# The output mixing of a hybrid block: its products in another order, its attention half in three rounded terms, and the first queries at its end

## The reference

```python
h = rms_norm(x, norm1_g);  proj = h @ w_in
y_lru = rg_lru(conv(xr)) * gelu(gate)              # 512 columns
y_fox = forgetting_attention(q, k, v, log_f)       # 512 columns, 8 heads
y_mix = concat(rms_norm(y_lru, gn_lru_g), rms_norm(y_fox, gn_fox_g))
x  = x + y_mix @ w_out                             # the mixing
h2 = rms_norm(x, norm2_g)
x  = x + peer(h2, peer_wq, peer_subkeys, peer_u, peer_v)
return rms_norm(x, final_g)
```

## Time and profile before

| what | value |
|---|---|
| median of 3 runs | 2812.67 us (2809.37 to 2816.16) |
| the profiled execution, whole | 2814.05 us |
| its span in the trace | 2812.3 us |
| PE busy in the span | 2706.6 us, 96% |
| DVE / ACT / POOL busy | 2306.2 / 1250.8 / 1456.7 us |
| instructions | 39998 |
| mixing block, start to the next block's first product | 476.8 to 608.2 us |
| score block, likewise | 608.2 to 830.6 us |

### The profile page before, as it was taken

How to read it: one execution, slowest core, us unless ns; L and a number is a source line. 1 busy time by engine, 2 the same in 40 slices (tenths; PEclk the granted TensorE clock), 3 DMA queues, 4 the chain that set the end, 5 groups by cost and what they waited for, 6 DMA issues and landing times. The chain is left out here.

```text
span 2812.3 us, 39998 instructions
## 1 busy us (share of the span) xinstructions
PE 2706.6 (96%) x14923; PEld 2374.2 (84%) x14923; DVE 2306.2 (82%) x4081; ACT 1250.8 (44%) x2540; POOL 1456.7 (52%) x935
## 2 busy tenths in 40 slices
PE   7999899979999999999999999989999999999998
PEld 6777665459999999999999999987788888878887
DVE  3297795329989989788979797775999999999997
ACT  4244432113332222888888888862222222222222
POOL 1122320004338885566666666662666666657662
PEclk9999899989999999999999999999999999999999
DMA  4110100323238886999999999999999999999995
GB/s 119 44 38 23 60 1 23 90 68 111 63 94 312 297 296 207 358 389 378 388 380 401 380 390 396 389 378 325 382 383 383 386 388 386 386 379 379 391 384 223
DMA packets 332114, 762.66 MB, mean 271 GB/s; under 512 B 23232, under 2 KB 158400, under 8 KB 329360
## 3 DMA queue, kind: packets, MB, share of 16 engines
q0 software_dynamic: 111104, 403.02, 38.3%
q1 hardware_dynamic: 220096, 353.67, 35.5%
q10 hardware_dynamic: 720, 3.41, 0.3%
HBM read 667.73 MB, written 92.27 MB: 270 GB/s over the span
## 5 line engine op out<-in xcount | busy, mean ns | idle before, releaser
L1985 POOL DMA_INDIRECT v_rows<-in_peer_v,row_numbers x336 | 535.6, 1594 | 332.5 <-DVE y_rest L2058 189.2
L1620 PE MATMUL expert_pre<-h2T,wq_then_uT_hi 128*128 128x320 f32 x4096 | 674.1, 314 | 24.5 <-ACT wq_then_uT_hi L1654 22.2
L1734 POOL DMA_INDIRECT u_rows<-in_peer_u,row_numbers x384 | 554.0, 1443 | 246.8 <-DVE row_weights L1754 161.0
L1620 PEld LDWEIGHTS expert_pre<-h2T,wq_then_uT_hi 128*128 128x128 f32 x4096 | 613.0, 189 | 27.3 <-issue 26.9
L2115 PE MATMUL expert_out<-v_hi,w_hi 128*128 128x512 f32 x1280 | 501.2, 392 | 12.7 <-DVE w_lo L2036 12.3
L1754 DVE CUSTOM_DVE_ANT_0 u_rows<-u_rows,h_rows_kept 128x1024 f32<-128x1024 f32 x384 | 488.3, 1300 | 27.8 <-DMA u_rows<-in_peer_u,row_numbers 27.7
L2115 PE MATMUL expert_out<-v_lo,w_hi 128*128 128x512 f32 x1280 | 499.6, 390 | 0.0
L2115 PE MATMUL expert_out<-v_hi,w_lo 128*128 128x512 f32 x1280 | 499.2, 390 | 0.0
L2058 DVE SCALAR_TENSOR_TENSOR y_rest<-v_rows,row_weights,y_rest 128x1024 f32<-128x1024 f32 x256 | 326.4, 1278 | 22.0 <-DMA v_rows<-in_peer_v,row_numbers 20.7
L1620 PE MATMUL expert_pre<-h2T,wq_then_uT_lo 128*128 128x320 f32 x2048 | 343.8, 310 | 0.6 <-POOL wq_then_uT_lo L1723 0.6
L1620 PEld LDWEIGHTS expert_pre<-h2T,wq_then_uT_lo 128*128 128x128 f32 x2048 | 312.4, 189 | 1.0 <-POOL wq_then_uT_lo L1723 0.8
(11 more groups left out here) (325 smaller groups left out, 4177.8 us busy)
## 6 DMA issues: line engine op xcount, KB each, us to landing
wq_then_u<-in_peer_u_turned SPq DMA_DIRECT2D x128, 512.0 KB
pick_memory<-in_peer_v SPq DMA_DIRECT2D x128, 512.0 KB
pick_memory<-acts_dram SPq DMA_DIRECT2D x128, 320.0 KB
acts_dram<-expert_acts SPq DMA_DIRECT2D x124, 320.0 KB
pick_memory<-gates_dram SPq DMA_DIRECT2D x31, 1280.0 KB
gates_dram<-pick_memory SPq DMA_DIRECT2D x19, 2048.0 KB
wq_then_u<-in_peer_wq SPq DMA_DIRECT2D x32, 512.0 KB, 4.0
w_in_columns<-in_w_in SPq DMA_DIRECT2D x20, 512.0 KB, 3.9
```

The source lines that it names most:

```text
L1620: last = nc.tensor.matmul(pre[:, (2 * c + half) % 4, 0:WIDTH], part[:, c % 2, k], m.h2T[:, t, k, HALVES[half]], start=n == 0, stop=n == le ...
L1734: pool.indirect_dma_start(rows[:, k % RING], None, table, bass.IndirectOffsetOnAxis(ap=m.row_of[:, f, slot:slot + 1], axis=0)).then_inc(fe ...
L1985: pool.indirect_dma_start(rows[:, k % ROW_RING], None, d.peer_v, bass.IndirectOffsetOnAxis(ap=m.row_of[:, f, slot:slot + 1], axis=0)).then ...
```

## The change

It gives the two halves different kinds of products, and moves work between three stages:

- The logits' three banks and the bank of the square sums become one PSUM tile of four banks, `m.front`, which the mixing and then the queries use too.
- `w_out` is loaded in attention in two halves. The second half goes to `m.rows`. In the mixing it is split there into `w_hi` (ACT) and `w_lo` (DVE 3 quarters, POOL 1), and then rows of x and new rows take its place.
- PE computes lru(0) in attention's end: 7 of its 8 products ahead of the last square sums, the last one behind them.
- The attention half of each tile is rounded by ACT (`split_fox`) and its rest taken by DVE (`low_fox`), in one buffer each. `out_fox` is then 24 rounded products instead of 8 plain ones.
- The lists of PE, DVE and ACT are interleaved one tile apart instead of two for fox, and the queries 0 and 1 on tiles 0 to 2 are made in the mixing's last two steps. POOL and SP split and load a third group of `peer_wq` there.
- The scores begin with query 2, the subkeys, scores 0 and 1, then query 3.

```diff
 @attend
+                def first_lru(products):
+                    if 0 in products:
+                        pe.wait_ge(m.w_out_in, 32)
+                        pe.wait_ge(gained, CT + 1)
+                        pe.wait_ge(logit_read, turn(FH, 0))
+                    for n in products:
+                        half, c = divmod(n, CT)
+                        last = nc.tensor.matmul(m.front[:, half], m.gateT[:, c, 0:P], m.w_out[:, c, half * HALF:(half + 1) * HALF],
+                                                start=c == 0, stop=c == CT - 1)
+                    return last
...
+                first_lru(range(2 * CT - 1))
                 pe.wait_ge(squared, SUMS)
                 square_sums(squares[:, (SUMS - 1) % 2], 2 * NT)
+                first_lru([2 * CT - 1]).then_inc(m.lru_mixed, 1)
 @mix_out, SP
+                sp.dma_start(gain2[:], d.norm2_g.partition_broadcast(P)).then_inc(m.gains_in, 16)
+                for n in range(2):
+                    sp.dma_start(m.wq[:, n], d.peer_wq[:, n * P:(n + 1) * P].rearrange("(k p) n -> p k n", p=P)
+                                 ).then_inc(m.wq_in[n], 16)
                 for b in range(NT):
-                    if b >= 2:
+                    if b < 2:
+                        m.w_out_lo_done.wait(sp, b + 1)
+                    else:
                         sp.wait_ge(dve4, added(b - 2, X2))
                     sp.dma_start(x_row[:, b % 2], d.x[b * P:(b + 1) * P, :]).then_inc(x_in[b % 2], 16)
...
+                sp.wait_ge(m.wq_lo_done, 1)
+                sp.dma_start(m.wq[:, 0], d.peer_wq[:, 2 * P:3 * P].rearrange("(k p) n -> p k n", p=P)).then_inc(m.wq_in[0], 16)
 @mix_out, ACT
+                def split_fox(b):
+                    if b:
+                        act.wait_ge(fox_mixed, b)
+                    A(fox_hi[:], fox_of(b), ACT.Copy).then_inc(m.fox_hi_done.semaphore, 1)
+
+                act.wait_ge(m.w_out_in, 32)
+                for c in range(CT):
+                    A(w_hi[:, c], m.rows[:, c], ACT.Copy).then_inc(m.w_out_hi_done.semaphore, 1)
+                split_fox(0)
                 act.wait_ge(dve4, 2)
                 A(rgroup[:], rgroup[:], ACT.Sqrt).then_inc(group_root, 1)
                 for b in range(NT):
+                    if b + 1 < NT:
+                        split_fox(b + 1)
                     act.wait_ge(dve4, added(b, X2))
...
 @mix_out, DVE
+                for c in range(BY_DVE):
+                    m.w_out_hi_done.wait(dve, c + 1)
+                    v.tensor_tensor(*split_of(c)).then_inc(m.w_out_lo_done.semaphore, 1)
+                low_fox(0)
...
-                add_groups(0)
-                add_groups(1)
+                add_lru(0)
+                add_lru(1)
+                add_fox(0)
                 for b in range(NT):
+                    if b + 1 < NT:
+                        low_fox(b + 1)
                     normalize(b)
+                    if b + 2 < NT:
+                        add_lru(b + 2)
                     low(b)
-                    if b + 2 < NT:
-                        add_groups(b + 2)
+                    if b + 1 < NT:
+                        add_fox(b + 1)
 @mix_out, PE
+                def mix_fox(b):
+                    m.fox_lo_done.wait(pe, b + 1)
+                    if b == 0:
+                        m.w_out_hi_done.wait(pe, CT)
+                        m.w_out_lo_done.wait(pe, BY_DVE)
+                        m.w_out_lo_pool.wait(pe, CT - BY_DVE)
+                    else:
+                        pe.wait_ge(dve4, added(b - 1, X2))
+                    terms = [(a, of, c) for a, of in ((fox_hi, w_hi), (fox_lo, w_hi), (fox_hi, w_lo)) for c in range(CT)]
+                    for half, cols in enumerate(halves(2)):
+                        for n, (a, of, c) in enumerate(terms):
+                            last = nc.tensor.matmul(out_fox[:, half], a[:, c], of[:, c, cols],
+                                                    start=n == 0, stop=n == len(terms) - 1)
+                    last.then_inc(fox_mixed, 1)
...
-                for b in range(2):
-                    mix_lru(b)
-                    mix_fox(b)
+                mix_lru(1)
+                mix_fox(0)
                 for b in range(NT):
                     if b + 2 < NT:
                         mix_lru(b + 2)
+                    else:
+                        query_of_rows(b + 2 - NT)
                     turn(b)
-                    if b + 2 < NT:
-                        mix_fox(b + 2)
+                    if b + 1 < NT:
+                        mix_fox(b + 1)
 @score, PE
-                for n in range(HP):
+                query_of(2)
+                turn_keys()
+                score_of(0)
+                score_of(1)
+                for n in range(3, HP):
                     query_of(n)
-                    if n == 0:
-                        turn_keys()
-                    else:
-                        score_of(n - 1)
+                    score_of(n - 1)
 @score, ACT
+                query_out(0)
+                query_out(1)
+                split_high(3)
+                for g in range(HP // 4):
+                    act.wait_ge(keys_turned, g + 1)
+                    A(keysT[:, 4 * g:4 * g + 4, :], keys_ps, ACT.Copy).then_inc(keysT_done, 1)
+                scores_out(0)
+                query_out(2)
+                scores_out(1)
+                split_high(4)
```

More of the change, by code:

```diff
@@ L57, in enter, with __init__, wait @@
         self.count, self.base = 0, i * per_pass
+class Counted:
+    def __init__(self, semaphore, base):
+        self.semaphore, self.base = semaphore, base
+    def wait(self, engine, count):
+        engine.wait_ge(self.semaphore, self.base + count)
 def halves(n=2):
@@ L1047, in _, with add_lru @@
                 dve.wait_ge(m.gains_in, 16)
-                def add_groups(b):
+                def add_lru(b):
                     s = b % 2
                     dve.wait_ge(lru_mixed, b + 1)
+                    if b == 0:
+                        m.w_out_lo_done.wait(dve, BY_DVE)
+                    if b == 1:
+                        m.w_out_lo_pool.wait(dve, CT - BY_DVE)
                     dve.wait_ge(x_in[s], 16 * (b // 2 + 1))
@@ L1070, in normalize @@
                     own.link(v.reciprocal(r2[:, b:b + 1], r2[:, b:b + 1]))
[L1071 to L1072 removed]
+                    if b:
+                        dve.wait_ge(h2_turned, b)
                     own.link(v.scalar_tensor_tensor(out=h2_of(b), in0=x2[:, s], scalar=r2[:, b:b + 1],
@@ L1088, in _, with mix_lru @@
-                assert own.count == normalizing(NT)
+                    assert own.count == lowered(b)
+                    if b + 1 < NT:
+                        add_fox(b + 1)
             @block.tensor
             def _(pe):
-                pe.wait_ge(m.w_out_in, 16)
-                def mix(b, to, of, first, which, done):
-                    if b:
-                        pe.wait_ge(dve4, added(b - 1, which))
+                def mix_lru(b):
+                    if b >= 2:
+                        pe.wait_ge(dve4, added(b - 1 if b > 2 else 0, LRU_READ))
@@ L1110, in turn, with query_of_rows @@
                     last.then_inc(h2_turned, 1)
-                for b in range(2):
-                    mix_lru(b)
-                    mix_fox(b)
+                def query_of_rows(n):
+                    pe.wait_ge(m.wq_lo_done, n + 1)
+                    pe.wait_ge(dve4, max(lowered(F - 1), added(NT - 1, LRU_READ)))
+                    terms = [(w, part, k) for w, part in ((m.wq_hi, 0), (m.wq_hi, 1), (m.wq_lo, 0)) for k in range(KT)]
+                    for i, (w, part, k) in enumerate(terms):
+                        last = nc.tensor.matmul(m.front[:, n, 0:F * P], w[:, n % 2, k], m.h2_of_rows[:, part, k],
+                                                start=i == 0, stop=i == len(terms) - 1)
+                    last.then_inc(m.query_done, 1)
+                mix_lru(1)
+                mix_fox(0)
                 for b in range(NT):
@@ L1312, in _ @@
                 sp.dma_start(keys[:], d.peer_subkeys.rearrange("h n c -> n h c")).then_inc(keys_in, 16)
-                for s in range(2, 2 * HP):
+                for s in range(3, 2 * HP):
                     sp.wait_ge(lo_done, s - 1)
@@ L1437, in scores_out @@
                     A(to[:, h % ring, p], score_ps[:, s % 2, tiles.start:tiles.stop], ACT.Copy).then_inc(scores_read, 1)
-                for n in range(HP):
-                    query_out(n)
-                    if n == 0:
-                        for g in range(HP // 4):
-                            act.wait_ge(keys_turned, g + 1)
-                            A(keysT[:, 4 * g:4 * g + 4, :], keys_ps[:], ACT.Copy).then_inc(keysT_done, 1)
-                    else:
-                        scores_out(n - 1)
+                query_out(0)
[8 more added lines that the diff above has]
+                split_high(4)
+                for n in range(3, HP):
+                    query_out(n)
```

(8 more changed lines are left out.)

110 lines of the change are left out of this document (64 added, 46 removed).

## The result

The changed kernel takes **2787.24 us** (median of 4 runs, 2781.68 to 2789.16), the kernel before 2814.01 beside it on the same chip: ratio **0.9905, 95% interval 0.9888 to 0.9922**. The forecast was 2787.0, range 2779 to 2798. The profiled execution took 2781.68 us with a span of 2779.9.

A forecast was written before the change was run, and what follows sets the result against it. PE's list was taken to set the mixing's and score block's ends. From 2814.05 us, 20.0 from the mixing and 6.4 from the scores, 26.4 together, gave 2787.6, stated as 2787 us, range 2779 to 2798.

The forecast's parts named there:

- Attention's end: End of attention: 7 plain products take 6.0 us in PE's wait, square sums 1.8; mixing starts at 476.5 instead of 476.85.
- Entry: Start of the mixing: ACT, DVE and POOL split weights and first tile beside lru(1), so fox(0) starts on time, 0.3 us spare.
- Rounded products: Mixing: 24 rounded products at 0.229 us make fox 5.5 us, 1.37 less than before; bounds 5.4 and 5.6.
- rival of equal passes: Mixing: each rounded product takes 0.2145 us, fox 5.15, eight give 2.8 us more, total 2784; chance 0.08.
- The tile's chain: Mixing, per tile: PE can turn 4.8 us after fox ends, other engines' work is covered, PE sets a period of 13.24.
- splits on the path: Mixing: each fox waits for round and rest, 2.3 us seven times, 16 us of the gain lost, 2803; chance 0.12.
- late store: Mixing: the new rows' store holds DVE, costing from a 9.1 us landing; over 13.5 gives 2815 and more; chance 0.02.
- Mixing block: Mixing from 476.5 to the score block's start at 588.2 instead of 608.22, a gain of 20.0 us.
- Start of the scores: Score block: query 3 ends 23.0 us after the start instead of 29.4, a gain of 6.4; bounds 4.0 to 8.8.
- the 5.1 from the first copy to score 0: Score block: from ACT's first copy of keys at 10.2 us to the next product takes 5.1, so score 0 starts at 15.3.
- The 2.3 for the slow clock behind the keys: Score block: 2.3 us added for PE's slow clock after resting between key rounds, on top of 1.2 and 4.25 at full clock.

The follow-up runs named there:

- lru_back: Changed kernel with lru(0) again at the head of the mixing instead of in attention's end: 2795.10 us, ratio 0.9930 to the kernel before.
- split_by_dve: Changed kernel with the rest of the fourth quarter of the weights taken by DVE instead of POOL: 2787.92 us, ratio 0.9915 to the kernel before.
- plain_fox: Changed kernel with the attention half again as 8 plain float32 products per tile, the splits left in place: 2796.88 us, ratio 0.9937 to the kernel before.
- store_four: Changed kernel with each of the first six stores of new rows done four times one after the other: 2813.38 us, ratio 1.0003 to the kernel before.
- second profile: The changed kernel run and profiled once more, nothing edited: 2784.48 us, ratio 0.9905 to the kernel before.
- queries_back: Changed kernel with queries 0 and 1 made in the score block, in the order of the kernel before: 2799.07 us, ratio 0.9948 to the kernel before.
- split_last: Changed kernel with ACT's split of weight group 3 behind the four copies of turned keys instead of ahead: 2786.04 us, ratio 0.9897 to the kernel before.
- warm_mid: Changed kernel with ACT's group 3 split between second and third key copies, plus three unread PE products before the first and after each of three key rounds: 2784.50 us.
- all_three: Changed kernel with the group 3 split between second and third key copies, unread products between key rounds, and the fourth weights' rest on DVE: 2783.91 us, ratio 0.9898.

## Why the prediction held, and where its steps were off

The mechanism was right: PE's list sets the time, its waits are filled, and the period is the one forecast. That the total is met to 0.2 us (2787.0 for 2787.2) is luck, since single runs of the kernel lie between 2781.7 and 2789.2. Block by block the first profile gives 0.4 in attention, 19.1 in the mixing and 5.6 in the scores, 25.1 for the 26.4 forecast, and the second 26.9; the two misses of 0.6 and 0.8 us below lie inside the spread.

- **Attention's end** held: 6.0 us of products, sums 1.84 for 1.8, 10.0 us to the mixing. `lru_back` gives its worth as a step of its own: 7.9 in the medians, 9.7 in the blocks.
- **Entry**: the step that failed is "DVE takes ... the tile's, about 0.7 ... POOL takes the fourth, 2.36". Side by side they took 2.84 and 2.89. DVE was in its third rest until 482.0, and POOL's subtraction, begun at 481.40, is longer by 0.54; then DVE's next one lasts until POOL is through; POOL's cast behind it is longer by 0.46. So each seems to have been held up by what the other had begun. `split_by_dve` shows that POOL's subtraction is the cause. The forecast had DVE done 5.6 us after the start of the mixing; it was done after 7.4, later than POOL. The Trainium skill, "SBUF — State Buffer", section "Who interferes with whom", says that a DVE instruction with two SBUF inputs contends with a GpSimd (here POOL) instruction that reads SBUF, and calls the port pair that they share an exclusive lock. These rows agree with it: 484.84, where the rest of fox ends, less its 0.69 is 484.15, within 0.14 of the end of POOL's subtraction at 484.29.
- **Rounded products**: 5.55 for fox, between the 5.5 taken and the upper bound 5.6; the period 13.21 for 13.24, the turn being 0.80 and not 0.87. The rival of equal passes (5.15) is out. `plain_fox` shows that this is what the middle gained.
- **The tile's chain** held: the last turn comes 4.80 after fox(7)'s end (580.89 to 585.69), as reckoned, and store, round and rest are covered. The rivals of splits on the path and of a late store did not happen; `store_four` shows that the second is real and its break-even well placed. The point from which it costs was put too low: rows free 9.7 us after the issue cost nothing, where 9.1 had been named, since PE needs the addition only at the next lru product. The price per late us was put too low as well, since the lru products behind the longer waits run slower (27.9 us longer with 18.5 of waits); the two errors nearly cancel.
- **Mixing block**: 112.26 for 111.7 (588.2 - 476.5), the 0.6 being the entry, fox(0) 7.44 after lru(1)'s start for 6.87.
- **Start of the scores**: ACT's first copy 10.1 for 10.2, and the reason, the late load of the weights, was the right one. Query 3 ended at 23.8 for 23.0. The term mis-sized is the 5.1 from the first copy to score 0: it took 6.0, because key rounds 2 to 4 took 1.80 each, where in the kernel before only the last did and the others took 1.34. The 2.3 for the slow clock behind the keys was right in sum and wrong in place: scores 0 and 1 took 1.4 more than the 1.2 named and query 3 0.9 more than 4.25. In the second profile the load landed 0.7 earlier and query 3 ended at 22.0. The bounds, 4.0 to 8.8 for 6.4, held with 5.6 and 7.4.
- **The three together**: `queries_back` shows a worth that the forecast had not named, 3.4 us in the mixing: a filled place in PE's list keeps the clock for the work behind it. It did not show in the sum because the turns and fox(7) had been priced at nearly the full rate anyway.

Open is why the expert stages, which nothing here touches, vary from 1973 to 1988 us between profiles, and how much of a gain in the score block reaches the end. With that spread the runs here can't tell. Open is also what decides when the clock falls among the key rounds.

## What to carry to other kernels

Price a wait of the busiest engine together with what the work behind it will cost, and fill it with products that are due anyway: here filling a wait of 5.3 us gave 7.9, and two moved queries gave 3.4 us in the mixing besides the 4.8 in the score block. Where a wait is new but hidden, work out from which duration it decides and test that by lengthening it: a longer landing that costs nothing shows the slack, and one that costs everything shows the break-even. When two engines subtract side by side, look at their single rows, not at a mean: both were longer by about what was left of the other's. And compare a small gain with every profile that leaves its stage alone, not with the first: of the 3.3 us that one order seemed to give, 2.0 lay within their spread.

## What the runs showed of the hardware that was not expected

- DVE's 128x512 subtraction from two SBUF tiles took 0.69 us alone and 2.84 (2.83 in `lru_back`) beside a POOL subtraction that had begun 0.6 before it.
- After waits of PE of 4.6 us the eight transposes took 1.62 instead of 0.80 and the first rounded products 0.46 each instead of 0.23 (half the clock). Four key rounds with gaps of 0.69 us between them all took 0.66 us in `split_last`; the last of them took 1.11 in the kernel before and in `queries_back`. Behind a gap of 2.73 the second round took 1.11 in one profile of the changed kernel and 0.66 in the other. With three unread products in each gap the clock stayed at 1.00 in `warm_mid` and fell to 0.64 among the rounds in `all_three`; the scores behind ran at 1.00 in both.
- A 512 KB store issued with a 512 KB load of x beside it landed in 5.2 us; the same store alone, right behind it, in about 2.6 (4.4 once); four in a row in 12.9 to 13.9.
